# First norm and router of a two-layer decoder step: sums taken in the output projection, a gather in fp32, 16 KB rows

## What is computed

```
h = LN1(alpha*x + concat(heads) @ w_o)
g = top1(softmax(h @ w_r1 + b_r1))                 # 4 groups
e = top2(softmax(h @ w_r2[g] + b_r2[g]))           # 4 experts in the group
y = sum over the 2 experts of gate * (silu(h @ w_gate) * (h @ w_up)) @ w_down
x = LN2(alpha*h + y)
LN(x) = (x - mean) / sqrt(mean((x - mean)^2) + 1e-5) * g + b
```

## Time and profile before

| | |
|---|---|
| median of three runs | 2639.15 us |
| the profiled execution | 2636.69 us |
| its span in the trace | 2634.8 us |
| TensorE busy | 2403.7 us, 91% of the span |
| VectorE / ScalarE / GpSimd busy | 637.6 / 521.8 / 61.9 us |
| mean granted TensorE clock | 0.947 |
| moved by DMA | 647.68 MB |

### The profile page before, as it was taken

The page is one execution under the profiler, slowest core; times in us unless marked ns, Lnnn a source line. Parts: engine busy times, 40 slices in busy tenths (PEclk is TensorE's granted clock), DMA queues, the critical chain, the costliest instruction groups (busy, mean ns, idle before and its releaser), DMA issues.

```text
span 2634.8 us, 32435 instructions
## 1 busy us (share of the span) xinstructions
PE 2403.7 (91%) x12635; PEld 1457.9 (55%) x12635; DVE 637.6 (24%) x1157; ACT 521.8 (20%) x1138; POOL 61.9 (2%) x60
## 2 busy tenths in 40 slices
PE   6899999999859999999989998999994999998997
PEld 4658886578533434343458876645872334444344
DVE  0209960420252121212120000032016112121213
ACT  1230014520321101010130014633004101010104
POOL 0000000000030000000000000000004000000000
PEclk9999999999959999999999998998996799999998
DMA  8503456794208999989835445997530498989890
GB/s 270 168 1 134 154 161 187 239 336 141 83 0 341 365 411 365 411 360 411 334 98 167 144 162 193 362 354 268 183 128 0 163 417 359 418 354 418 354 383 33
DMA packets 251065, 647.68 MB, mean 246 GB/s; under 512 B 56825, under 2 KB 90250, under 8 KB 216890
## 3 DMA queue, kind: packets, MB, share of 16 engines
q1 hardware_dynamic: 215578, 636.28, 63.9%
q10 hardware_dynamic: 35376, 9.91, 1.6%
HBM read 640.16 MB, written 5.96 MB: 245 GB/s over the span
## 4 chain that ended last, share of the span: by engine, by line
PE 77%; DMA 12%; ACT 4%; DVE 2%; ACTq 2%; issue 1%; POOL 1%; SPq 0%; POOLq 0%; DVEq 0%
PE bank L597 16%; PE bank L1068 11%; PE bank L1178 9%; PE bank L1052 8%; PE bank L1098 7%; DMA ring<-in_w_down 6%; DMA ring<-in_w_up 5%; PE bank L1112 4%; PE bank L772 4%; PE bank L781 2%; PE bank L912 2%; ACT arena L1199 2%; ACTq L377 1%; PE bank L674 1%; PE bank L697 1%
## 5 line engine op out<-in xcount | busy, mean ns | idle before, releaser
L1199 ACT ACTIVATE arena<-bank 128x512 f32<-128x512 f32 (+5 forms) x585 | 293.1, 549 | 1011.2 <-PE bank L597 415.2
L1068 PE MATMUL bank<-ring,AT 128*64 128x512 f32 x2048 | 454.8, 603 | 27.2 <-DMA ring<-in_w_up 25.4
L597 PE MATMUL bank<-X,ring 128*128 128x264 f32 x1664 | 374.3, 388 | 1.2 <-ACT arena L1199 1.2
L597 PEld LDWEIGHTS bank<-X,ring 128*128 128x128 f32 x1664 | 318.2, 191 | 56.3 <-ACT arena L1199 1.4
L1068 PEld LDWEIGHTS bank<-ring,AT 128*64 128x64 f32 x2048 | 148.0, 139 | 325.5 <-issue 292.4
L1098 PE MATMUL bank<-ring,arena 128*64 128x512 f32 x1024 | 235.0, 616 | 41.8 <-DMA ring<-in_w_down 33.7
L1052 PE MATMUL bank<-arena 128*128 128x256 bf16 (+1 forms) x1440 | 221.2, 301 | 20.8 <-POOL arena L548 20.8
L1178 PE MATMUL bank<-AT,ring 128*128 128x264 f32 x1024 | 231.8, 390 | 0.0
L1178 PEld LDWEIGHTS bank<-AT,ring 128*128 128x128 f32 x1024 | 197.0, 193 | 34.2
L1881 DVE TENSOR_TENSOR X<-bank,X 128x264 f32<-128x264 f32 x256 | 110.7, 433 | 406.9 <-PE bank L1112 404.0
L1052 PEld LDWEIGHTS bank<-arena 128*128 128x128 bf16 (+1 forms) x1440 | 122.4, 103 | 123.6 <-issue 84.1
(11 more groups left out here) (250 smaller groups left out, 1510.0 us busy)
## 6 DMA issues: line engine op xcount, KB each, us to landing
ring<-in_w_gate SPq DMA_DIRECT2D x64, 2048.0 KB, 17.8
ring<-in_w_up SPq DMA_DIRECT2D x64, 2048.0 KB, 13.2
ring<-in_w_down SPq DMA_DIRECT2D x64, 2048.0 KB, 16.7
ring<-in_w_o SPq DMA_DIRECT2D x16, 2048.0 KB, 9.9
ring<-in_cache_b_k SPq DMA_DIRECT2D x128, 256.0 KB, 4.3
ring<-in_cache_b_v SPq DMA_DIRECT2D x128, 256.0 KB, 4.9
ring<-in_w_in_a SPq DMA_DIRECT2D x14, 2048.0 KB, 9.0
ring<-in_w_in_b SPq DMA_DIRECT2D x12, 2048.0 KB, 8.4
```

Source lines behind the costliest of these rows:

```text
L597: mm = pe.matmul(B[4 * (g % 2) + f][:, 0:n_tok], u[:, c * 512 + f * P:c * 512 + (f + 1) * P], src[8 * half + c][:, 0:n_tok], start=(half = ...
L1068: mm = pe.matmul(B[bank][64 * s:64 * s + 64, :], M.xsT[:, at:at + 64], ring[slots[s][0]][:, c * FE:(c + 1) * FE], start=(half == 0 and c = ...
L1199: return act.activation(out, in_, ACT.Copy, scale=scale)
```

## The change

All in the stage from the output projection to the loop, and in how experts' weights lie in a slot:

- A shift `M.sh`, the mean of the first 12 blocks, is taken after half 0 of the last slab and subtracted from all; what is left of the mean is summed over blocks 12 to 15 alone (bank 3) and taken off afterwards, in the variance, in the logits and, as `shift`, in the blocks.
- The squares' sums of blocks 0 to 11 and raw logits (bank 2, weights `wr` times g, made once as `M.wrg`) are matmuls between the column groups of the last half slab; blocks 12 to 15 follow it. 16 small matmuls after the first half slab (`router_sums`) give the sums of `wr*g` and `wr*b` with which VectorE finishes the logits; slab 1 waits until VectorE has read them (`sums_read`), behind slab 0's `mix`.
- The blocks are shifted and normalised in four parts (`normalise`) inside `route`: ahead of the logits' copy, ahead of each of the two waits for an exponential, and after `chosen`.
- Square buffers: four for two, in both norms. ScalarE asks for its tables by a one-column activation ahead of the squares (Sqrt) and after the root (Exp).
- Token rows are kept in fp32 and copied once by ScalarE; GpSimd's part is gone. The gather is 48 fp32 matmuls for 144 in bf16; `M.sel` is fp32.
- A unit of `w_gate`, `w_up` or `w_down` is one contiguous 2 MB run, 16 KB for each partition. `down` goes over row blocks outside and the four banks inside, so that a bank is complete only in the last quarter; `hidden` writes in the order that fits.

```
 # GpSimd
-                for n in range(1, 14):
-                    ...   # rest = rest - high ; low = rest - mid, 12 items each
 # SyncE
-   src = w.rearrange("a (g p j) f -> p (a g) (j f)", p=P, j=4)[:, 2 * half:2 * half + 2, :]
+   src = w.rearrange("a (g p j) f -> p (a g) (j f)", p=P, j=8)[:, half:half + 1, :]
-   src = w.rearrange("a (c p) f -> p (a c) f", p=P)[:, :, D // 2 * half:D // 2 * (half + 1)]
+   src = w.rearrange("a (g p j) f -> p (a g) (j f)", p=P, j=2)[:, half:half + 1, :]
 # TensorE
+            def squares(k, cs, logits=False):
+                for c in cs:
+                    pe.wait_ge(S("ln_square"), 16 * k + c + 1)
+                    pe.matmul(B[1][:, 0:T], cst("mean"), M.sq[c % 4], ...).then_inc(S("ln_square_used"), 1)
+                    if logits:
+                        mm = pe.matmul(B[2][0:20, 0:T], M.wrg[:, 20 * c:20 * c + 20], Xc[c], ...)
+            def mix(layer):
+                for k in range(4):
+                    for half in range(2):
+                        u = arrived(pe, layer, "o", 2 * k + half)
+                        if k == 1 and half == 0:
+                            pe.wait_ge(S("sums_read"), layer + 1)
+                        for f in range(4):
+                            ...   # 8 matmuls, as before
+                            if k == 3 and half == 1 and f < 3:
+                                squares(k_ln, range(4 * f, 4 * f + 4), True)
+                        if k == 0 and half == 0:
+                            router_sums(layer)
+                        if k == 3 and half == 0:
+                            pe.wait_ge(S("mixed"), 12 * (layer + 1))
+                            for c in range(12):
+                                mm = pe.matmul(B[0][:, 0:T], cst("mean"), Xc[c], ...)
+                            mm.then_inc(S("ln_mean"), 1)
+                for c in range(12, KC):
+                    pe.wait_ge(S("ln_centred"), 16 * k_ln + c + 1)
+                    pe.matmul(B[3][:, 0:T], cst("mean"), Xc[c], ...)
+                    squares(k_ln, [c], True)
             def experts(layer):
-                for c in range(KC):   # logits from Xc, after ln_out
-                    ...
+                for q in range(3):
+                    token_rows(layer, q)
                 pe.wait_ge(S("chosen"), layer + 1)
                 ...   # ranks
+                token_rows(layer, 3)
+                pe.wait_ge(S("token_rows_copied"), 12 * (layer + 1))
                 # gather
-                                for k in range(3):
-                                    mm = pe.matmul(B[2 + q % 4][...], M.part[t][k][...], M.sel[...], ...)
+                                mm = pe.matmul(B[2 + q % 4][...], M.xtok[0:rows, at:at + P], M.sel[...], ...)
 # VectorE, mix: after slab 0 router_weights (M.wrg, two 20x1 reads of bank 7); then
+                link(dve.tensor_scalar(M.sh, B[0][:, 0:T], KC / 12.0, None, ALU.mult))
+                for c in range(12):
+                    dve.tensor_tensor(Xc[c], Xc[c], M.sh, ALU.subtract).then_inc(S("ln_centred"), 1)
+                for c in range(12, KC):
+                    link(dve.scalar_tensor_tensor(Xc[c], Xc[c], ALPHA, M.sh, ALU.mult, ALU.subtract))
+                left(dve, layer, "o", 7)
+                for c in range(12, KC):
+                    dve.tensor_tensor(Xc[c], Xc[c], B[c - 8][:, 0:T], ALU.add).then_inc(S("ln_centred"), 1)
+                dve.wait_ge(S("ln_sums"), layer + 1)
+                ...   # copy of bank 3, its square, variance, + eps (4 linked operations)
+                shift(layer, 0)
+                dve.wait_ge(S("ln_std"), k_ln + 1)
+                link(dve.reciprocal(M.rstd, M.rstd))
+                ...   # three operations on 20x264 finish the logits
+            def normalise(layer, q):
+                if q:
+                    shift(layer, q)            # 4 subtractions
+                for c in range(4 * q, 4 * q + 4):
+                    dve.tensor_tensor(Xc[c], Xc[c], M.rstd, ALU.mult).then_inc(S("ln_normed"), 1)
 # ScalarE, experts
+                affine(2 * layer, range(0, 4))
+                router_exp(0)
+                affine(2 * layer, range(4, 8))
+                row_copies(layer, 0)
+                router_exp(1)
+                affine(2 * layer, range(8, 12))
+                row_copies(layer, 1)
+                row_copies(layer, 2)
+                affine(2 * layer, range(12, 16))
+                row_copies(layer, 3)
```

More of the change, by code:

```diff
@@ L292, in step_kernel @@
         at = 0
[L294 to L312, removed]
+        M.xtok = ar(at, 3 * D); at += 3 * D
         M.lgT = ar(at, T, 20); at += T
@@ L317, in step_kernel @@
         M.c1 = [ar(at + 3 * k, 3) for k in range(12)]; at += 36
+        at = lay[1].memK_at
+        assert 3 * D + 648 <= at
+        M.xsT = AT[:, 0:KC * 2 * P]
+        at += 2048
+        M.ex = ar(at, 512); at += 512
+        M.hh = ar(at, 512); at += 512
+        M.hT = ar(at, 512); at += 1024
+        M.ys = ar(at, D); at += D
+        M.sel = ar(at, 6 * P); at += 6 * P
+        M.sg = ar(at, 6 * P); at += 6 * P
+        M.sq = [ar(at + T * k, T) for k in range(4)]
+        M.rstd = ar(at + 4 * T, T)
+        M.ind = ar(at, (ENTRIES - NE) * NE * CHUNKS)
+        assert (ENTRIES - NE) * NE * CHUNKS <= 3 * T
+        M.gt = [ar(at + (3 + k) * T, T) for k in range(2)]; at += 5 * T
+        M.sh = ar(at, T); at += T
+        M.wrg = ar(at, KC * 20); at += KC * 20
+        M.lb = ar(at, 4, 20); at += 4
         M.cnt = ar(at, 16); at += 16
@@ L379, in row_item @@
         def row_item(n):
-            t, q = divmod(n - 1, 4)
+            q, t = divmod(n, 3)
             rows = P if t < 2 else NB
-            return rows, t, [M.part[t][k][0:rows, 512 * q:512 * (q + 1)] for k in range(3)]
+            g, h = divmod(q, 2)
+            block = M.xtok[0:rows, t * D + 1024 * g:t * D + 1024 * (g + 1)].rearrange("r (j p) -> r j p", j=8)
+            return q, t, rows, block[:, :, 64 * h:64 * (h + 1)]
         block = ctx.enter_context(nc.Block())
@@ L984, in layer_norm, with router_sums @@
                 mm.then_inc(S("ln_mean"), 1)
+                squares(k, range(KC))
+            def router_sums(layer):
+                pe.wait_ge(S("wr_copied"), layer + 1)
                 for c in range(KC):
-                    pe.wait_ge(S("ln_square"), 16 * k + c + 1)
-                    pe.matmul(B[1][:, 0:T], cst("mean"), M.sq[c % 2], start=(c == 0), stop=(c == KC - 1))\
-                      .then_inc(S("ln_square_used"), 1)
+                    g = 16 * layer + c
+                    mm = pe.matmul(B[7][0:20, 0:2], wr[:, 20 * c:20 * c + 20], lnp[:, g:g + 33:32],
+                                   start=(c == 0), stop=(c == KC - 1))
+                mm.then_inc(S("router_sums"), 1)
@@ L994, in router_weights, with last_rows @@
                 leave(mm, layer, "r")
-            def token_rows(tiles, last):
-                for t in tiles:
+            def last_rows():
+                for t in range(3):
                     rows = P if t < 2 else NB
                     for q in range(4):
[L1001 to L1004, removed]
+                        n = 4 * t + q + 1
+                        if n > 4:
+                            pe.wait_ge(S("token_rows_copied"), 24 + n - 4)
+                        if t == 0:
                             pe.wait_ge(S("ln_out"), 3 * KC + 4 * q + 4)
@@ L1402, in layer_norm @@
                        .then_inc(S("ln_out"), 1)
+            def layer_norm(k):
+                squares(k)
+                affine(k, range(KC))
             def token_rows():
@@ L1561, in _ @@
                      B[6][:, 0:320].rearrange("p (j a c) -> p c a j", a=5, c=KC)).then_inc(S("wr_copied"), 1)
-                layer_norm(2 * layer)
+                squares(2 * layer)
                 experts(layer)
@@ L1761, in route @@
                 dve.tensor_tensor(gp, lg[:, :, 0:4], b3(mx, 4), ALU.subtract).then_inc(S("r_shifted"), 1)
+                normalise(layer, 1)
                 dve.wait_ge(S("r_exp"), 2 * layer + 1)
@@ L1776, in route @@
                 dve.tensor_tensor(ep, el, b3(mx, 4), ALU.subtract).then_inc(S("r_shifted"), 1)
+                normalise(layer, 2)
                 dve.wait_ge(S("r_exp"), 2 * layer + 2)
@@ L1799, in route @@
                 dve.sem_inc(S("chosen"), 1)
+                normalise(layer, 3)
                 dve.wait_ge(S("ranks"), layer + 1)
```

216 lines of the change are left out of this document (114 added, 102 removed).

## The result

The changed kernel is slower: 2693.9 us (2690.5 to 2695.2, four runs) against 2635.9 for the kernel before in the same comparison, ratio 1.0207 with a 95% interval from 1.0189 to 1.0225. The forecast was 2582. Most of the mechanisms came as forecast; one term, the price of a gather in fp32, was wrong by more than all gains together.

The account below looks back on a forecast made before the run. Bound: a serial chain over all engines before each layer's first gather, then a loop through TensorE and DMA. Per layer -14.8 - 11.5 - 3.0 = -29.3, loop 0: -58.6, rounded to -57, giving 2580, as median 2582; range 2562 to 2612.

Parts of the forecast that it names:

- the first gather and its copies in the loop: 48 fp32 matmuls a gather: the first takes 22.5 us for 34.00, gain 11.5 a layer; those in the loop 20.7 for 19.05.
- Cold gather: Rival: the first fp32 gather runs at 1.2 GHz throughout, +18.9 us a layer, 2620 in all; chance 14%.
- Router: From logits to ranks: with GpSimd's operations gone VectorE's small operations get short, gaining 8.8 us a layer.
- From ranks to gather: Stretch between the ranks and the first gather: 8.9 us for 18.0, token rows last; gain 9.1 a layer.
- Second norm: Four square buffers let the squares follow TensorE, 7.1 us for 10.16: -3.0 for each of two.
- Ring rows: Expert weights' transfers in the loop: 16 KB rows give 427 GB/s and save 1.9 us a quad.
- Late banks of `down`: In the loop: `down` completing its banks late costs nothing, as the last bank ends when it did.
- Projection, norm and logits: Start of each layer's stage, up to VectorE's logits: a loss of 3.1 us, 719.2 against 716.09.
- the rival that was slower than before: Rival: 16 KB rows slow the DMA queue to 387 GB/s, 8.1 us a quad more, 2647 in all; chance 4%.

Follow-up runs that it names:

- kernel 2: The changed kernel with the third token tile gathered over all 128 rows, the added ones zeroed, so no changes of tile size: 2588.2 us, ratio 0.9791.
- kernel 8: The kernel before with the third tile of the three bf16 parts zeroed and gathered over 128 rows: 2572.5 us, ratio 0.9753.
- kernel 1: The changed kernel with the gather's token tiles reordered, so tile size changes 16 times a gather instead of 32: 2633.8 us, ratio 0.9984 to the kernel before.
- kernel 3: The changed kernel with 29 dense, thrown-away matmuls a layer in TensorE's gaps between the last sums and the first gather, 32 changes kept: 2648.1 us, ratio 1.0038.
- kernel 5: The changed kernel with only the gather's arithmetic undone: 144 bf16 matmuls, lower two parts a zeroed tile, GpSimd's splitting still gone: 2600.9 us, ratio 0.9866.
- Kernel 10: The kernel before with fp32 rows copied once, no GpSimd splitting and the fp32 gather over full rows; first norm as it was: 2583.6 us, ratio 0.9789.
- kernel 6: The kernel before with only the 16 KB rows, `down` over row blocks and the matching order of features: 2627.1 us, ratio 0.9951.
- kernel 9: On kernel 4, each group's squares first and then its logits matmuls, where they alternated: 2567.7 us, ratio 0.9732.
- kernel 4: The changed kernel with both the third token tile gathered over full 128 rows and 29 dense matmuls a layer ahead of the first gather: 2574.4 us, ratio 0.9745.

## Why the prediction was wrong

**The step that failed is the first gather and its copies in the loop, costed by the wrong row.** The prediction took 0.432 us for a 256-column fp32 matmul from a stage in which all tiles are alike, and multiplied by 48. In this gather every third matmul has 8 rows, and each change of tile size costs 0.19 us in fp32 (26.98 - 20.93 = 6.05 us over 32, by kernel 2), 0.100 in bf16 (19.05 - 15.84, by kernel 8). At full clock a gather is 6.3 us longer than forecast; eight of the ten are in the loop and, as the prediction said, paid in full. The two first ones took 50.50 for 22.5, for these changes and for the clock. 8 x 6.3 + 2 x 28.0 = 106 us, of the 112 between forecast and measurement. The clue stood in the trace: the old gather's 0.132 us a matmul was a mean over matmuls of two sizes, and weight loads on the timeline show 0.21 us of idle time at each boundary. The prediction took the 19.05 us whole, without taking them apart. The Trainium skill has a rule that may be behind this ("TensorEngine Tiling (Array Packing)", Key Properties): changing the tiling mode drains TensorE. It gives no price, and no run here shows that a tile of 8 rows changes the mode; the time lost at each boundary in kernels 1, 2 and 8 agrees with it.

**The clock.** "Cold gather" was a rival with 14%, and it came. The argument against it, that all fp32 work had come back to full clock, was true of work without changes of tile size. The runs order it: entering at half clock, the fp32 gather stayed there for 50.5 us with 32 changes, rose after some 19 us with 16, and after 5 us with none, in both layers each time. Between 32 and 16 nothing else differs; with none there are also more rows. What came ahead counts too: behind dense matmuls it rose after 1.9 us with all 32 (kernel 3), and once up the clock stayed. And the changes do not fix the moment: with 32 of them the bf16 gather rose after 33.4 us or not at all in the kernel before, after 22.7 or not at all in kernel 5. Whether it is the changes themselves or the short idle times that they bring, no run separates. The Trainium skill's rule ("TensorE: Matmul & The Clock Gate", Part 1), that sustained busy time raises the clock, is too short for the changed kernel: TensorE was busy 10.00 of 10 us at 0.50, by the profile, whose busy time is modelled and takes in the time lost at the changes. The rival was priced at +19 a layer, without the changes, which cost 0.27 us each at half clock ((50.50 - 2 x 20.93)/32); it was +28.

**What was right.** *Router*: VectorE's operations went from up to 1.09 to 0.17 us, and from the logits' reading to the gather passed 23.7 us, for 42.8; the prediction had 24.9. Kernel 10 shows where they come from: 12.9 us from reading to ranks without the split into parts, 24.8 with it, with norm and logits as before. Of these 11.9 us, 10.0 are twelve VectorE operations that took 0.81 to 1.09 us for 0.17, and 1.9 are a shorter wait for ScalarE's first exponential (2.43 for 4.32), ahead of which ScalarE had waited for GpSimd. From ranks to gather the prediction had the token rows last; in the chain it is VectorE's selection matrix, at 7.9 us for 8.9. The Trainium skill ("SBUF — State Buffer", Who interferes with whom) lets a VectorE operation with two SBUF inputs contend with GpSimd's reads; the trace agrees: all twelve have two inputs, while those with one stayed at 0.17 and 0.18 us beside GpSimd (L1756, L1785). *Second norm*: -3.0, as forecast. *Ring rows*: the rate is 430 to 434 GB/s where 427 was extrapolated, the gain 11 us for 15. *Late banks of `down`*: no cost seen; kernel 6 carries them and is faster.

**Right in sign, wrong in size.** *Projection, norm and logits*: a loss of 3.1 us was forecast and 7.0 measured. `router_sums` cost 0.96 us and not 4.2, the wait 2.3 and not 2.6; but the alternation of 128 and 20 columns, again a change of tile size, cost some 3.6 (kernel 9) and was not in the sum, and the projection's own 512 records took 118.4 us for the 115.6 in the sum. 1.7 of that lie behind the new wait: the prediction let 2.6 us of idleness leave the clock alone, and after 2.33 it was at 0.57 from 599.8 to 603.0. With the normalising, which does stand in VectorE's chain, the whole move costs 9 us a layer (kernel 10).

**The balance.** With the gather near its forecast price the time is 2574 (kernel 4, with matmuls ahead that the change did not have) or 2588 (kernel 2, without them), and 2582 was forecast. The range, 2562 to 2612, left out even the cold gather at 2620; no rival had the gather itself dearer than its matmuls, and the rival that was slower than before was put on the DMA queue, which became faster instead.

## What to carry to other kernels

Count changes of tile size (rows or columns of the stationary) as instructions of their own: 0.10 us in bf16, 0.19 in fp32 for rows and 0.15 for columns here. Zero-padding a short tile to full rows was cheaper here than switching to it, and grouping alike tiles next best. A row's mean is a price only for the same sequence of shapes: divide it by the bare column time first and explain the rest. A stage that meets TensorE at half clock and has such changes may stay there to its end; either take out the changes or give it something dense to do just ahead. And test the parts of a change singly: here the rows copied once in fp32 paid and the moved sums of the norm did not.

## What had not been expected of the hardware

With identical matmuls and data, halving the number of changes ended the stretch at 1.2 GHz after 19 us, where it had lasted all of 50.5 (kernel 1). In the kernel before, half of the 34 us of each layer's first gather were this: padding alone, which adds rows to a third of its matmuls, brought it from 34.0 to 17.25 us and that kernel from 2638.1 to 2572.5. And 32 fp32 records with 2 moving columns take 0.96 us, 0.03 each, far less than the 0.13 of records with 8 columns and wide stationaries.
